# Value stage with half of its tile pairs as seven block products, token weights stationary, on one core

## What is computed

```
q = (xb @ w_query).reshape(TB, PH, 2, PEER_QUERY_DIM // 2)
...                                    # 16 best of 16384 experts per head and token
g = jax.nn.softmax(top_s, axis=-1).astype(xb.dtype)
u = expert_u[idx]
a = jax.nn.gelu(jnp.einsum('td,thkd->thk', xb, u), approximate=False)
return jnp.einsum('thk,thkd->td', g * a, expert_v[idx])
```

## Time and profile before

| | us |
|---|---|
| median of 3 runs | 974.62 |
| the profiled execution: its own time | 976.8 |
| the profiled execution: span of the trace | 974.9 |
| TensorE busy | 962.2 |
| DVE busy | 756.8 |
| ACT busy | 559.6 |
| POOL busy | 339.2 |
| in 612 to 955 (value stage): TensorE, DVE, ACT, POOL busy | 343.0, 256.8, 169.6, 20.1 |

### The profile page before, as it was taken

The page is one execution under the profiler, slowest core; times in us unless marked ns, Lnnn a source line. Parts: engine busy times, 40 slices in busy tenths (PEclk is TensorE's granted clock), DMA queues, the critical chain, the costliest instruction groups (busy, mean ns, idle before and its releaser), DMA issues.

```text
span 974.9 us, 23876 instructions
## 1 busy us (share of the span) xinstructions
PE 962.2 (99%) x8425; PEld 942.3 (97%) x8425; DVE 756.8 (78%) x1604; ACT 559.6 (57%) x996; POOL 339.2 (35%) x199
## 2 busy tenths in 40 slices
PE   9999999999999999999999999999999999999997
PEld 9989899999999999999999999999999999999997
DVE  7988868879799977687777675777777777677765
ACT  6456854666655647676677664555455455444544
POOL 0000000077877868888888880010001000000000
PEclk9999999999999999999999999999999999999999
DMA  8877677756577889999999998999999999899871
GB/s 306 258 223 205 194 204 233 232 179 215 190 231 232 253 251 287 264 258 300 290 266 293 274 274 258 337 323 319 302 316 312 346 290 310 265 306 290 271 241 45
DMA packets 134083, 254.60 MB, mean 261 GB/s; under 512 B 29856, under 2 KB 78880, under 8 KB 133744
## 3 DMA queue, kind: packets, MB, share of 16 engines
q1 hardware_dynamic: 112048, 235.30, 75.1%
q0 software_dynamic: 21376, 17.12, 8.4%
q10 hardware_dynamic: 576, 1.06, 0.3%
HBM read 227.07 MB, written 26.35 MB: 260 GB/s over the span
## 4 chain that ended last, share of the span: by engine, by line
PE 86%; DVE 5%; DMA 4%; issue 2%; ACT 2%; SPq 0%; POOL 0%; ACTq 0%; DVEq 0%
PE pO L1415 38%; PE pTT L1714 18%; PE pM L1714 17%; PE pO L1694 6%; DMA raw<-in_stream 3%; DVE wlos L905 2%; PE pSS L1480 1%; DMA a_scratch<-ast 1%; PE pSS L1740 1%; PE pSS L1636 1%; PE pTT L1669 1%; ACT whis L642 1%; PE pSS L1669 1%; PE pM L1519 0%; DMA xcol<-in_xcol 0%
## 5 line engine op out<-in xcount | busy, mean ns | idle before, releaser
L642 ACT ACTIVATE whis<-raw 128x1024 fp32r<-128x1024 f32 x326 | 345.2, 1059 | 235.1 <-PE pM L1714 171.2
L1415 PE MATMUL pO<-xhi,whis 128*128 128x240 f32 (+1 forms) x1040 | 288.5, 277 | 0.8 <-DVE wlos L905 0.8
L1415 PE MATMUL pO<-xlo,whis 128*128 128x240 f32 (+1 forms) x1040 | 285.9, 275 | 0.0
L1415 PE MATMUL pO<-xhi,wlos 128*128 128x240 f32 (+1 forms) x1040 | 285.9, 275 | 0.0
L905 DVE TENSOR_TENSOR wlos<-raw,whis 128x1024 fp32r<-128x1024 f32 x173 | 209.9, 1218 | 18.4 <-ACT whis L642 16.7
L1319 DVE TENSOR_TENSOR wlos<-raw,whis 128x1024 fp32r<-128x1024 f32 x125 | 153.2, 1225 | 86.6 <-ACT whis L642 74.0
L622 POOL DMA_INDIRECT g_scratch<-small x112 | 205.0, 1830 | 37.9 <-issue 33.5
L1415 PEld LDWEIGHTS pO<-xhi,whis 128*128 128x128 f32 x1040 | 196.2, 189 | 3.5 <-issue 2.0
L1415 PEld LDWEIGHTS pO<-xlo,whis 128*128 128x128 f32 x1040 | 196.4, 189 | 0.0
L1415 PEld LDWEIGHTS pO<-xhi,wlos 128*128 128x128 f32 x1040 | 196.3, 189 | 0.0
L583 POOL TENSOR_TENSOR wlos<-raw,whis 128x1024 fp32r<-128x1024 f32 x29 | 70.0, 2422 | 215.4 <-ACT whis L642 215.4
(11 more groups left out here) (285 smaller groups left out, 1879.9 us busy)
## 6 DMA issues: line engine op xcount, KB each, us to landing
raw<-in_stream SPq DMA_DIRECT2D x199, 512.0 KB
raw<-in_vrows SPq DMA_DIRECT2D x128, 512.0 KB
a_scratch<-ast SPq DMA_DIRECT2D x128, 120.0 KB
held<-a_scratch SPq DMA_DIRECT2D x128, 120.0 KB, 4.6
g_scratch<-ghot SPq DMA_DIRECT2D x32, 256.0 KB, 4.4
held<-x_scratch SPq DMA_DIRECT2D x16, 512.0 KB
held<-g_scratch SPq DMA_DIRECT2D x124, 64.0 KB, 4.4
biasm<-in_bias SPq DMA_DIRECT2D x8, 256.0 KB, 5.4
```

The lines of the kernel that those rows point to most:

```text
L642: act.activation(whi[s], raw[s][:], ACT.Copy).then_inc(hi_ready, 1)
L1415: last = pe.matmul(dst, st, mv, start=(c == 0 and q == 0), stop=(c == len(terms) - 1 and q == 2))
```

## The change

The value stage keeps the token weights stationary (128 experts by 128 tokens) and moves V, 512 columns at a time, into token rows. All 256 tokens take part; the 16 apart tokens stay apart in the expert stage only, where all their 16 dot products are now done, so that nothing is gathered from V. The tiles are taken in 32 groups of four. In groups 1 to 30 the first two tiles form a "mixed" pair: token weights as 2 x 2 blocks (tiles x token halves), V as 2 x 2 blocks (tiles x halves of the 1024), and their product as seven block products (Strassen's scheme in Winograd's form) into seven sums, of which four have PSUM banks of their own (`mixed`). The other two tiles, and all of groups 0 and 31, are plain: 12 matmuls of 512 columns a tile.

The block products need sums of blocks, and each sum needs its high and low part. So DVE computes per group: three instructions of V sums (`value_sums`), six of the mixed weights (`mix_weights`), two of the plain pair's weights (`plain_weights`), and four subtractions for low parts (`mix_low`, `sums_low` twice, `plain_low`). The low parts of V itself, which DVE wrote before, are written by POOL (`base_low`), in one half and three whole tiles of 1024 per group. ACT rounds all of them (`highs`).

Around it: the output is in token rows, so the closing transposes go; the residual is kept in token rows, for which the query stage transposes it (16 transposes); the table build has 32 steps instead of 28; seven sums are added to the residual by DVE (`add_bank`) before the last four tiles are multiplied in five pieces.

```diff
+G_STEPS = P // GTOK
...
+            def base_low(g, s, half=False):
+
+                pool.wait_ge(base_hi[s], g)
+                part = slice(0, 1 if half else 2)
+                pool.tensor_tensor(quarter_lo[:, s, part], quarter[:, s, part], quarter_hi[:, s, part].bitcast(F32), ALU.subtract).then_inc(base_lo[s], 1)
+
+            def lows(g):
+
+                base_low(g + 1, 0, True)
+                base_low(g + 1, 1)
+                base_low(g + 1, 2)
+
+            lows(0)
+            with pool.Fori(1, PAIRS_G - 2) as g:
+                base_low(g, 3)
+                lows(g)
+            base_low(PAIRS_G - 2, 3)
+            for s in range(3):
+                base_low(PAIRS_G - 1, s)
...
+            def base_high(g, s, half=False):
+
+                act.wait_ge(raw_landed[s], (g + (T_V // 4 + 1)) * 16)
+                act.wait_ge(base_done[s], g)
+                part = slice(0, 1 if half else 2)
+                act.activation(quarter_hi[:, s, part], quarter[:, s, part], ACT.Copy).then_inc(base_hi[s], 1)
...
+            def highs(g, mix_side, plain_side, early=False):
+
+                base_high(g + 1, 0, True)
+                base_high(g + 1, 1)
+                mix_high(g + 1, mix_side, not early)
+                sums_high(g + 1, 0, t13_made, t13_done, t13_hi, not early)
+                sums_high(g + 1, 2, t24_made, t24_done, t24_hi, not early)
+                if early:
+                    act.wait_ge(w_made[1], g + 2)
+                    act.wait_ge(base_done[1], 1)
+                    act.activation(wplain_hi[plain_side], wplain, ACT.Copy).then_inc(plain_hi, 1)
+                else:
+                    next_plain_high(g + 1, plain_side)
+                base_high(g + 1, 2)
 
...
+            def weights(g, q, dst):
+
+                p = g * 2 + q
+                mine = G[:, :, p * 2:p * 2 + 2] if isinstance(p, int) else G[:, :, bass.ds(p * 2, 2)]
+                dve.wait_ge(a_landed[q], (g + 1) * 16)
+                dve.tensor_tensor(dst[:, A21:A22 + 1:A22 - A21, :], apair[q][:, :, P:T], mine.rearrange("p t o -> p o t"), ALU.mult)
...
+            def mix_weights(g):
+
+                if not (isinstance(g, int) and g == FIRST_W):
+                    dve.wait_ge(mix_lo, g - 1)
+                weights(g, 0, wmix)
+                dve.wait_ge(w_made[0], g + 1)
+                dve.tensor_tensor(wmix[:, S3, :], wmix[:, A11, :], wmix[:, A21, :], ALU.subtract).then_inc(s3_made, 1)
+                dve.tensor_tensor(wmix[:, S1, :], wmix[:, A22, :], wmix[:, A21, :], ALU.add)
+                dve.wait_ge(s3_made, g)
+                dve.tensor_tensor(wmix[:, S2, :], wmix[:, A22, :], wmix[:, S3, :], ALU.subtract).then_inc(s2_made, 1)
+                dve.wait_ge(s2_made, g)
+                dve.tensor_tensor(wmix[:, S4, :], wmix[:, A12, :], wmix[:, S2, :], ALU.subtract).then_inc(s4_made, 1)
+
+            def mix_low(g, side):
+
+                dve.wait_ge(mix_hi, g)
+                dve.tensor_tensor(wmix_lo[side][:, A11:], wmix[:, A11:], wmix_hi[side][:, A11:].bitcast(F32), ALU.subtract).then_inc(mix_lo, 1)
+
+            def value_sums(g):
+
+                for s in range(2):
+                    dve.wait_ge(raw_landed[s], (g + (T_V // 4 + 1)) * 16)
+                if not (isinstance(g, int) and g == FIRST_W):
+                    dve.wait_ge(t13_lo, g - 1)
+                    dve.wait_ge(t24_lo, g - 1)
+                dve.tensor_tensor(vsum[:, 0:2, :], quarter[:, 0:2, 1, :], quarter[:, 0, :, :], ALU.subtract).then_inc(t13_made, 1)
+                dve.wait_ge(t13_made, g)
+                dve.tensor_tensor(vsum[:, 2, :], vsum[:, 1, :], quarter[:, 0, 0, :], ALU.add).then_inc(t2_made, 1)
+                dve.wait_ge(t2_made, g)
+                dve.tensor_tensor(vsum[:, 3, :], quarter[:, 1, 0, :], vsum[:, 2, :], ALU.subtract).then_inc(t24_made, 1)
+
+            def sums_low(g, first, high, ready):
+
+                dve.wait_ge(high, g)
+                at = slice(first, first + 2)
+                dve.tensor_tensor(vsum_lo[:, at, :], vsum[:, at, :], vsum_hi[:, at, :].bitcast(F32), ALU.subtract).then_inc(ready, 1)
+
+            def parts(g, mix_side, plain_side, last=False):
+
+                value_sums(g + 1)
+                if isinstance(g, int) and g == 0:
+                    mix_weights(1)
+                mix_low(g + 1, mix_side)
+                plain_weights(g + 1, 1, g + 3)
+                sums_low(g + 1, 0, t13_hi, t13_lo)
+                sums_low(g + 1, 2, t24_hi, t24_lo)
+                plain_low(g + 3, plain_side)
+                if not last:
+                    mix_weights(g + 2)
...
+            def add_bank(at, bank):
+
+                n = at.shape[1]
+                return dve.tensor_tensor(at, bank.unsqueeze(1).to_broadcast([P, n, 512]), at, ALU.add)
+
+            link(add_bank(four, mixed[0]))
+            link(add_bank(four[:, 1:4, :], mixed[2]))
+            link(add_bank(four[:, 2:4, :], mixed[3]))
+            add_bank(four[:, 1:4:2, :], mixed[1]).then_inc(mixed_taken, 1)
+            dve.wait_ge(mixed_taken, 1)
+            dve.wait_ge(base_hi[3], PAIRS_G - 1)
...
+            def mixed_pair(g, side, opening=False, closing=False):
+
+                pe.wait_ge(base_lo[0], g)
+                pe.wait_ge(mix_lo, g)
+                mixed_product(mixed[0], A11, side, quarter_hi[:, 0, 0, :], quarter_lo[:, 0, 0, :], opening, closing).then_inc(base_done[0], 1)
+                pe.wait_ge(base_lo[1], g)
+                mixed_product(acc[0][0], A12, side, quarter_hi[:, 1, 0, :], quarter_lo[:, 1, 0, :])
+                mixed_product(acc[0][1], S4, side, quarter_hi[:, 1, 1, :], quarter_lo[:, 1, 1, :]).then_inc(base_done[1], 1)
+                pe.wait_ge(t13_lo, g)
+                mixed_product(mixed[1], S1, side, vsum_hi[:, 0, :], vsum_lo[:, 0, :], opening, closing)
+                mixed_product(mixed[3], S3, side, vsum_hi[:, 1, :], vsum_lo[:, 1, :], opening, closing).then_inc(t13_done, 1)
+                pe.wait_ge(t24_lo, g)
+                mixed_product(mixed[2], S2, side, vsum_hi[:, 2, :], vsum_lo[:, 2, :], opening, closing)
+                mixed_product(acc[1][0], A22, side, vsum_hi[:, 3, :], vsum_lo[:, 3, :]).then_inc(t24_done, 1)
...
+            def v_tile(s, side, opening=False, closed=None):
+
+                for b in range(TB):
+                    for n, (st, mv) in v_terms(s, b, side):
+                        for q in range(2):
+                            last = pe.matmul(acc[b][q], st, mv[:, q, :], start=opening and n == 0, stop=n == 2 and (b, q) == closed)
+                last.then_inc(base_done[s], 1)
+
+            def plain_pair(g, n, side):
+
+                pe.wait_ge(plain_lo, n)
+                for s in range(2, 4):
+                    pe.wait_ge(base_lo[s], g)
+                    v_tile(s, side)
```

More of the change, by code:

```diff
@@ new lines, in _, with steady, steady_groups @@
+            load_third(2)
+            def steady(g):
+                load_last(g + 1)
+                load_parts(g + 1, 1)
+                load_first(g + 2)
+                load_parts(g + 2, 0)
+                load_third(g + 2)
+            def steady_groups(first, end):
+                with sp.Fori(first, end) as h:
+                    steady(h)
+            steady_groups(1, H_GROUP)
+            sp.wait_ge(base_done[0], 1)
+            sp.wait_ge(h1_stored, 16)
+            sp.dma_start(gf[:], gfin.to_broadcast([P, D])).then_inc(final_landed, 16)
@@ new lines, in _ @@
+            plain_high(2, 0)
+            highs(0, 1, 0, True)
+            base_high(1, 3)
+            act.wait_ge(s4_made, 2)
+            base_high(2, 0, True)
+            base_high(2, 1)
+            act.activation(wmix_hi[0][:, A11:], wmix[:, A11:], ACT.Copy).then_inc(mix_hi, 1)
+            sums_high(2, 0, t13_made, t13_done, t13_hi)
+            sums_high(2, 2, t24_made, t24_done, t24_hi)
+            next_plain_high(2, 1)
+            base_high(2, 2)
+            with act.Fori(0, (PAIRS_G - 4) // 2) as h:
+                for side in range(2):
+                    base_high(h * 2 + (2 + side), 3)
+                    highs(h * 2 + (2 + side), 1 - side, side)
@@ new lines, in _ @@
+            with dve.Fori(0, (PAIRS_G - 4) // 2 - 1) as h:
+                for side in range(2):
+                    parts(h * 2 + (2 + side), 1 - side, side)
+            for g in range(PAIRS_G - 4, PAIRS_G - 2):
+                parts(g, 1 - g % 2, g % 2, g == PAIRS_G - 3)
+            plain_weights(PAIRS_G - 1, 0, PAIRS_G + 1)
+            plain_low(PAIRS_G + 1, 0)
+            plain_weights(PAIRS_G - 1, 1, PAIRS_G + 2)
+            plain_low(PAIRS_G + 2, 1)
+            dve.wait_ge(final_landed, 32)
```

650 lines of the change are left out of this document (306 added, 344 removed).

## The result

The changed kernel takes 1176.11 us (median of four runs, 1174.50 to 1176.89) against 974.56 us (973.63 to 975.51), a ratio of 1.2066 with a 95% interval of 1.2045 to 1.2087. The profiled execution has a span of 1173.6 us.

A forecast was written before the change was run, and what follows sets the result against it. TensorE bounds the kernel before; after, DVE and POOL taking turns make 16.8 us a group. From 629, 29 groups (487) reach 1116, plus 35 for the end: 1151, rounded to 1150 us; range 1095 to 1210.

The forecast's parts named there:

- The three stretched instructions of DVE: Query stage before: DVE instructions of 0.48, 0.41 us took 2.54, 2.61, 2.08 beside POOL, taken as doing no work meanwhile.
- The group: Value stage, four tiles: DVE and POOL times add to 16.8 us, not TensorE's 10.1; range 15.4 to 18.3.
- DVE's 9.05: Value stage, per mixed group: DVE's fifteen instructions, 7,040 elements a partition, with strided reads and waits, sum to 9.05 us.
- POOL's 8.2: Value stage, per mixed group: POOL's 3.5 subtractions of 1024 at 2.34 us each take 8.2 us.
- a sign against it: Value stage: forecast is wrong if DVE's 1024-wide subtraction stays near 1.23 us beside POOL's 2.4 us.
- whole instructions: Value stage, upper case: whole DVE and POOL durations add, 18.3 us a group, end near 1195 us.
- third rival: Value stage: idle gaps drop TensorE's clock to 1.2 GHz, 45 matmuls take 19.2 us and bind, 1237 us; chance 5%.
- Ahead of the value stage: Before the value stage: transposes 1.8 us, table steps 1.9, zero matmuls gone; start at 611.8 + 3 = 615 us.
- The end: After the last mixed groups: plain pair, bank additions to 19.8, last pieces to 28.0, tail 7; sum 35 us.
- No exclusion: Value stage: DVE and POOL do not hold each other up, TensorE stays the bound, 952 us, 2.3% faster; chance 6%.
- the second rival: Value stage: no mutual holding, but DVE's chain, 9.05 us plus 2 us waiting for ACT's copies, 11.1 a group, 982 us; 3%.
- The fourth: Value stage: the change does not reduce columns, 23,040 per group before and after; called certain, already in the sum.

The follow-up runs named there:

- isolated pairs: Separate program, none of the layer: DVE and POOL subtractions of 1024 elements, SBUF only; eight on DVE alone 9.2 us, four on POOL 9.23, together 17.75.
- the spare work in the kernel before: Kernel before plus unread POOL subtractions in 27 groups of four tiles: four per group 1159.80 us (1.1874), one per group 981.86 us (1.0063).
- the run with one column: Changed kernel with POOL subtracting one column of each half V tile instead of 512, other V low parts left out: 997.86 us, 1.0228.
- the run with twelve dots packed: Changed kernel with four of the sixteen apart dot products left out, the twelve kept at their places in the changed kernel: 1169.69 us, 1.1975.

## Why the prediction was right

**The sign and the mechanism** held: 1150 was forecast, with 1095 to 1210, and 1176.11 came. The three stretched instructions of DVE in the query stage were enough to forecast the behaviour of a stage that the trace didn't contain. The isolated pairs show the exclusion, halving POOL's work and moving it to DVE show that it sets the group, and the spare work in the kernel before shows it without the change.

**The group**: 16.8 forecast, 17.02 measured, over 29 groups 6.3 us. DVE's 9.05 was 9.4 (11.07 less 1.5 of waits in the run with one column, and 0.2 of issue); with POOL's 8.2 that makes 17.6, so some 0.6 us pass side by side where 0.4 were taken off. These two misses offset each other in part, which is luck. The wait for A, 0.8 us a group, was not foreseen; in the group shown it lies under POOL's work. Nor was the ring through ACT that the run with fewer sums' low parts showed; it happens to be as long as the sum. That POOL alternates evenly with DVE was only half so: V sums and all but the end of the low parts of the sums run while POOL stands (mean 1220 ns at L1453), and the mixed weights take what POOL's block costs, where the text had DVE alone for them. The text named DVE's 1024-wide one near 1.23 us beside POOL as a sign against it; it stays there because next to nothing of POOL is beside it, and the sign was badly chosen. In the isolated pairs the same width takes 2285 ns in the mean. By the Trainium skill's whole instructions (SBUF — State Buffer, "SBUF: two separate sides") a group was 18.3 us; the trace has 17.02, and the isolated pair 17.75 where the two alone sum to 18.4.

**TensorE**: 76% busy for 60 to 70% forecast, waits of 3.9 us a group for 5.7. The difference is its clock. In the timeline of one group, the first matmul after the wait, two at half speed and two after the return:

```profile
810.68 0.76 PE L1879 MATMUL pO<-whis,wmix_hi 128*128 128x512 f32 x1 [4.12 <-DVE wmix_lo L1434]
811.25 0.63 PE L1879 MATMUL pO<-wlos,wmix_hi 128*128 128x512 f32 x1
811.67 0.63 PE L1879 MATMUL pO<-whis,wmix_lo 128*128 128x512 f32 x1
...
816.28 0.39 PE L1879 MATMUL pSS<-vsum_lo,wmix_hi 128*128 128x512 f32 x1
816.50 0.39 PE L1879 MATMUL pSS<-vsum_hi,wmix_lo 128*128 128x512 f32 x1
```

Starts are 0.43 us apart for twelve matmuls, 1.2 GHz, and then 0.23, 2.4 GHz; the granted clock is 0.80 in the window. The third rival's mechanism was there, but 12 x 0.2 = 2.4 us lie within what would else be TensorE's wait, and in the run with one column, where it has hardly such a gap, the clock was 0.99. In the run with twelve dots packed only six or seven matmuls were slow, the clock was 0.90 and the waits 5.0 to 5.4 us, and the group was 17.04 all the same. So the clock set the time nowhere but at the end. The Trainium skill (TensorE: Matmul & The Clock Gate, "HAM oscillation") lets such a gap throttle the engine each time, and the trace agrees, with the group at 17.02 us all the same.

**Ahead of the value stage** is the step that was mis-sized most: "The stage starts at 611.8 + 3 = 615" was 626, 11 of the 23 us by which the span exceeds 1151. The matmuls were counted, the moved dots were put at nothing on the ground that DVE has time: they cost 5.5 us, by the waits above through their DMAs, in a stage whose DMA share was 0.92. The steps' price of 1.9 fits the 2.2 measured, though one reading inside the scatter can't confirm it. The key scores end 2.5 us later for the transposes, priced 1.8. Of the 14.2 us by which the stage starts later than in the kernel before, these make 10.2; about 4 us, near the scatter of the starts, stay unexplained. The plain weights of group 1 end at 641.3 for 629; that is the start and 1.3 us.

**The end**: from the plain weights of the thirtieth group (1134.75) to the end 38.9 us for 35. The last plain low part came at 16.6 us for 13.2, the four banks took 6.6 as forecast, then TensorE had stood for 8.39 us and ran its first six matmuls 0.43 us apart, at 1.2 GHz, 9.9 us for 8.2; the tail took 5.7 for 7:

```profile
1158.06 0.80 PE L1927 MATMUL pTT<-whis,vhi 128*128 128x512 f32 x1 [8.39 <-DVE htok L1514]
```

Together 12.3 + 6.3 + 3.9 = 22.5 us on 1151 of span, and 1173.6 is what the trace has.

**The rivals.** No exclusion was forecast to give 952 us; the nearest run gave 997.9 with groups of 11.07 (10.1 forecast). There the estimate of the second rival, 11.1 a group, is the one that fits, and for its reason in part: DVE's chain, though its waits are for A and not for ACT. The fourth, that no column is saved, was in the sum.

## What to carry to other kernels

Add up, on each engine, what a change needs per group, and then add DVE and POOL to one number wherever both work on SBUF operands; here 9.4 and 8.2 us beside a TensorE of 10.1 made 17. One operand in PSUM on DVE's side takes an instruction out of that number. A single stretched instruction in the trace before can tell of it. What is left out of the sum comes out in full only as long as no ring of waits is as long: 2 us less on DVE gave 0.8. Moving a subtraction from POOL (2.3 us of the shared time) to DVE (1.15 us) is a gain in such a stage even when DVE is the busiest engine, and when a step is moved, its DMAs go with it and have to be priced too.
